# Gated-linear-attention heads in pairs and differential-attention maps in turns: matmuls that alternate between rows of the TensorE array

## The reference

```python
p = jax.nn.softmax(jnp.where(allowed, s, MASK_VALUE), axis=-1)
w = p[:, :, 0] - lam * p[:, :, 1]
return jnp.einsum('bhqk,bkhe->bqhe', w, v)
```

```python
decay = jnp.exp(jnp.where(causal[:, :, None], cum[:, :, :, None, :] - cum[:, :, None, :, :], NEG))
attn = jnp.einsum('bhik,bhjk,bhijk->bhij', qc, kc, decay)
o_intra = jnp.einsum('bhij,bhjv->bhiv', attn, vc)
...
merged = gates[:, :, 0, :] * (branches[0] @ w_branch[l, 0])
for n in range(1, N_BRANCH_2):
    merged = merged + gates[:, :, n, :] * (branches[n] @ w_branch[l, n])
```

## Time and profile before

| | |
|---|---|
| median of 3 runs | 2612.03 us (2608.58 to 2612.68) |
| the profiled execution | 2606.96 us, of which the span is 2605.2 us |
| PE matmul | 2459.5 us busy, 94% of the span, 18862 instructions |
| PE weight load | 2339.8 us, 90% |
| DVE | 1817.3 us, 70% |
| ACT | 1333.6 us, 51% |
| POOL | 419.9 us, 16% |
| mean granted TensorE clock | 0.972 |
| HBM read | 362.60 MB, 140 GB/s over the span |

### The profile page before, as it was taken

The page is one execution under the profiler, slowest core; times in us unless marked ns, Lnnn a source line. Parts: engine busy times, 40 slices in busy tenths (PEclk is TensorE's granted clock), DMA queues, the critical chain, the costliest instruction groups (busy, mean ns, idle before and its releaser), DMA issues.

```text
span 2605.2 us, 50262 instructions
## 1 busy us (share of the span) xinstructions
PE 2459.5 (94%) x18862; PEld 2339.8 (90%) x18862; DVE 1817.3 (70%) x3451; ACT 1333.6 (51%) x2218; POOL 419.9 (16%) x548
## 2 busy tenths in 40 slices
PE   7999998999999999998999998999999988999998
PEld 6998997888999998997888998888999988889998
DVE  5698855666875689856676774876766558667664
ACT  5644455755544644455755545544444454344443
POOL 0000003617930000003526940000000000000000
PEclk9999998999999999999999998988999999899999
DMA  5432342344554433342334554432545543334553
GB/s 208 161 107 100 112 147 88 114 138 146 170 171 156 167 113 109 106 146 98 114 133 151 171 178 138 146 114 90 170 158 182 186 140 128 101 118 146 195 186 130
DMA packets 100432, 366.76 MB, mean 141 GB/s; under 512 B 11632, under 2 KB 12144, under 8 KB 99824
## 3 DMA queue, kind: packets, MB, share of 16 engines
q1 hardware_dynamic: 100208, 363.69, 41.8%
HBM read 362.60 MB, written 1.05 MB: 140 GB/s over the span
## 4 chain that ended last, share of the span: by engine, by line
PE 58%; DVE 18%; POOL 9%; DVEq 5%; ACT 4%; issue 3%; ACTq 1%; DMA 1%; SPq 0%; POOLq 0%
PE psum L450 58%; POOL ring_lo L1963 9%; DVE ring_lo L1282 4%; ACT arena L852 2%; ACT ring_hi L865 1%; DVE arena L1316 1%; DVE arena L1324 1%; DMA ring<-w 1%; DVEq L1757 1%; DVE arena_r L1270 1%; DVEq L1262 1%; DVE arena_r L1268 1%; PE psum L527 1%; DVE arena L1414 1%; DVEq L1439 1%
## 5 line engine op out<-in xcount | busy, mean ns | idle before, releaser
L450 PE MATMUL psum<-hn_hi,ring_hi 128*128 128x272 f32 (+2 forms) x3936 | 1169.4, 298 | 46.6 <-ACT hn_hi L852 20.4
L450 PE MATMUL psum<-hn_hi,ring_lo 128*128 128x272 f32 (+2 forms) x3936 | 1138.3, 290 | 0.0
L450 PE MATMUL psum<-hn_lo,ring_hi 128*128 128x272 f32 (+2 forms) x3936 | 1103.4, 288 | 0.0
L450 PEld LDWEIGHTS psum<-hn_hi,ring_hi 128*128 128x128 f32 x3936 | 767.5, 195 | 79.8 <-issue 54.6
L865 ACT ACTIVATE ring_hi<-ring 128x1024 fp32r<-128x1024 f32 x684 | 715.0, 1055 | 231.0 <-DMA ring<-w 200.5
L1282 DVE TENSOR_TENSOR ring_lo<-ring,ring_hi 128x1024 fp32r<-128x1024 f32 x548 | 668.3, 1228 | 225.5 <-ACT ring_hi L865 187.0
L450 PEld LDWEIGHTS psum<-hn_hi,ring_lo 128*128 128x128 f32 x3936 | 767.3, 195 | 0.0
L450 PEld LDWEIGHTS psum<-hn_lo,ring_hi 128*128 128x128 f32 x3936 | 746.8, 193 | 1.7
L852 ACT ACTIVATE arena<-psum 128x272 f32<-128x272 f32 (+10 forms) x722 | 251.5, 366 | 707.9 <-PE psum L450 598.9
L1963 POOL TENSOR_TENSOR ring_lo<-ring,ring_hi 128x256 fp32r<-128x256 f32 x544 | 419.7, 808 | 1104.7 <-ACT ring_hi L865 1104.7
L450 PE MATMUL psum<-arena_r,ring_hi 128*128 128x256 f32 (+2 forms) x2996 | 555.2, 286 | 20.5 <-DVEq L1262 10.1
(11 more groups left out here) (154 smaller groups left out, 1463.7 us busy)
## 6 DMA issues: line engine op xcount, KB each, us to landing
ring<-w SPq DMA_DIRECT2D x684, 512.0 KB, 3.3
cst<-consts SPq DMA_DIRECT2D x1, 2120.0 KB, 14.6
x_sb<-x_meta SPq DMA_DIRECT2D x1, 1088.0 KB, 4.9
out<-x_sb SPq DMA_DIRECT2D x1, 1024.0 KB, 4.8
arena<-lam SPq DMA_DIRECT2D x1, 256.0 KB, 4.0
par_sb<-par SPq DMA_DIRECT2D x1, 193.0 KB, 4.8
pos_sb<-positions SPq DMA_DIRECT2D x1, 128.0 KB, 6.4
cst<-consts SPq DMA_DIRECT2D x1, 65.5 KB, 5.0
```

Source lines behind the costliest of these rows:

```text
L450: i = nc.tensor.matmul(out_, lhsT=lhsT, rhs=rhs, start=first, stop=last)
```

## The change

GLA's heads go in pairs. A new helper `side_by_side` takes the banks of both members first and then issues their matmuls in turns, part by part, so that neighbouring matmuls lie on different partitions. The merges move between the chunks: merge 4p after chunk 0 of both heads, merge 4p+1 after chunk 1 and the two cross products, merges 4p+2 and 4p+3 ahead of the two heads' values. ACT and DVE follow the same order; DVE calls `low` for merge 4p ahead of the first masked sum of a pair, and sums both heads' chunk 0, merges, then both heads' chunk 1. The scores of the first DSA head go ahead of merge 6 instead of merge 7. In the differential attention the two maps of a head take turns in the same way, the 16-row matmuls of both last. No matmul is added or left out. `level_parts` is `level_products` without the issuing.

```diff
+            def side_by_side(b, banks):
+                ps = [b.take(pe, key) for key, _ in banks]
+                for i in range(max(len(parts) for _, parts in banks)):
+                    for (key, parts), p in zip(banks, ps):
+                        if i < len(parts):
+                            rows, cols, lhsT, rhs = parts[i]
+                            mm(p[rows, cols], lhsT, rhs, True, True, b.filled(key) if i == len(parts) - 1 else None)
...
             def da_scores(h):
-                for m in range(2):
-                    q, k = DQ[64 * m:64 * m + 64, h, :], DK[64 * m:64 * m + 64, h, :]
-                    scores(b1, ("ds", h, m), [(slice(0, P), slice(0, P), q[:, 0:P], k[:, 0:P]),
-                                              (slice(0, P), slice(P, 3 * P), q[:, P:2 * P], k[:, 0:2 * P])])
-                    scores(b1, ("ds", h, 2 + m), [(slice(0, N_META), slice(0, T1), q[:, 2 * P:T1], k)])
+                maps = [(DQ[64 * m:64 * m + 64, h, :], DK[64 * m:64 * m + 64, h, :]) for m in range(2)]
+                side_by_side(b1, [(("ds", h, m), [(slice(0, P), slice(0, P), q[:, 0:P], k[:, 0:P]),
+                                                  (slice(0, P), slice(P, 3 * P), q[:, P:2 * P], k[:, 0:2 * P])])
+                                  for m, (q, k) in enumerate(maps)])
+                side_by_side(b1, [(("ds", h, 2 + m), [(slice(0, N_META), slice(0, T1), q[:, 2 * P:T1], k)])
+                                  for m, (q, k) in enumerate(maps)])
...
-                for g in range(GLA_HEADS):
-                    r = slice(32 * g, 32 * g + 32)
+                for p in range(GLA_HEADS // 2):
+                    pair = [(g, slice(32 * g, 32 * g + 32)) for g in (2 * p, 2 * p + 1)]
                     for t in range(2):
-                        level_products(b2, g, Z2[r, :, :], t, GQ[r, :], GK[r, :])
-                    scores(b2, ("cross", g), [(slice(0, P), slice(0, P), Z2[r, 3, 0:P], Z2[r, 3, P:T2])])
-                    merge2(0, 2 * g)
-                    if g == GLA_HEADS - 1:
+                        for n in range(2):
+                            side_by_side(b2, [level_parts(g, Z2[r, :, :], t, GQ[r, :], GK[r, :])[n] for g, r in pair])
+                        if t == 1:
+                            side_by_side(b2, [(("cross", g), [(slice(0, P), slice(0, P), Z2[r, 3, 0:P], Z2[r, 3, P:T2])]) for g, r in pair])
+                        merge2(0, 4 * p + t)
+                    if p == 1:
                         attention_scores("s", 0)
-                    merge2(0, 2 * g + 1)
-                    pe.wait_ge(*s2["att"].upto(g))
-                    values2("g", g, GV)
...
+                    for g, r in pair:
+                        merge2(0, 4 * p + 2 + g % 2)
+                        pe.wait_ge(*s2["att"].upto(g))
+                        values2("g", g, GV)
+                    sum_squares(b2, ("ssg", p), [SQ2[:, p, :]], T2, [s2["sqo"].upto(p)], ones64)
...
+                for p in range(GLA_HEADS // 2):
+                    pair = (2 * p, 2 * p + 1)
+                    low(b2, ("mB", 0, 4 * p), 2)
                     for t, cols in ((0, slice(0, P)), (1, slice(T2, T2 + P))):
...
+                        for g in pair:
...
+                            masked_sum(b2, ("lv", g, t), LT2, SS[:, g % 2, cols])
...
+                        merge_two(0, 4 * p + t)
+                    if p == 1:
                         attention_masked("s", 0)
...
+                    merge_two(0, 4 * p + 2)
+                    merge_two(0, 4 * p + 3)
```

More of the change, by code:

```diff
@@ L529, in transposes, with level_parts @@
                         t.then_inc(*b.filled(key))
-            def level_products(b, h, Zv, t, q, k):
+            def level_parts(h, Zv, t, q, k):
                 n = P if t < 2 else N_META
@@ L546, in level_products @@
                 if t < 2:
[L547 to L550, removed]
+                    return [(("lv", h, t, 0), parts[:1] + [part(0, 0, 64), part(1, 0, 32), part(1, 64, 32)] + parts[1:4]),
+                            (("lv", h, t, 1), parts[4:])]
+                return [(("lv", h, t, 0), parts)]
+            def level_products(b, h, Zv, t, q, k):
+                for key, parts in level_parts(h, Zv, t, q, k):
+                    scores(b, key, parts)
             def values_times_weights(b, key, V, base, cols, rows=slice(0, P), more=True):
@@ L1222, in _ @@
                 for g in range(GLA_HEADS):
[L1223 to L1224 removed]
+                    if g % 2 == 0:
+                        merge_sigmoid2(0, 2 * g)
+                        merge_sigmoid2(0, 2 * g + 1)
+                    merge_sigmoid2(0, 4 * (g // 2) + 2 + g % 2)
                     r = slice(64 * (g % 2), 64 * (g % 2) + 64)
@@ L1900, in _ @@
                         fence(s2["z"].done())
-                for g in range(GLA_HEADS):
-                    dve.wait_ge(*b2.full(("m", "o", 1) if g < 2 else ("g", "o", g - 2)))
+                for p in range(GLA_HEADS // 2):
+                    pair = (2 * p, 2 * p + 1)
+                    low(b2, ("mB", 0, 4 * p), 2)
                     for t, cols in ((0, slice(0, P)), (1, slice(T2, T2 + P))):
[L1905 to L1909, removed]
-                        attention_masked("s", 0)
[L1911 to L1921, removed]
@@ new lines, in _ @@
+                        for g in pair:
+                            if t == 0:
+                                dve.wait_ge(*b2.full(("m", "o", 1) if p == 0 else ("g", "o", g - 2)))
+                            masked_sum(b2, ("lv", g, t), LT2, SS[:, g % 2, cols])
+                            if t == 1:
+                                dve.wait_ge(*b2.full(("cross", g)))
+                                V.tensor_copy(SS[:, g % 2, P:T2], b2.of(("cross", g))[:, 0:P]).then_inc(*b2.free(("cross", g)))
+                                fence(s2["att"].done(g))
@@ new lines, in _ @@
+                        merge_two(0, 4 * p + t)
+                    if p == 1:
+                        attention_masked("s", 0)
+                    merge_two(0, 4 * p + 2)
+                    merge_two(0, 4 * p + 3)
+                    dve.wait_ge(*s2["rs"].upto(("ssg", p)))
+                    V.scalar_tensor_tensor(TP2[:, 1, 0:T2], GO[:, p, :], parb("ggla"), RS[:, 0:T2], ALU.mult, ALU.mult)
+                    V.drain()
+                    V.scalar_tensor_tensor(GG[:, p, :], GG[:, p, :], 0.5, TP2[:, 1, 0:T2], ALU.mult, ALU.mult)
@@ L1922, in _ @@
+                    V.drain()
+                    split(GG[:, p, :], GGS[0][:, p, :], GGS[1][:, p, :])
+                    fence(s2["normed"].done(p))
                 attention_combined("s", 0)
```

3 lines of the change are left out of this document (removed).

## The result

Before the change the runs timed beside it had a median of 2611.03 us (2608.58 to 2612.68, 4 runs), after it 2574.13 us (2570.13 to 2576.26, 4 runs). The ratio is 0.9859, with a 95% interval of 0.9844 to 0.9874: 36.9 us less. The prediction had 2573.5 us for the median and 2568.4 us for the profiled execution, which took 2575.9 us.

The account below looks back on a forecast made before the run. PE bounds the kernel with 58% of the chain of waits, DVE taking over in GLA once PE shortens. 2606.96 - 27.6 (GLA) - 11.0 (differential attention) = 2568.4 us profiled, plus 5.1 gives 2573.5 us median; range 2551 to 2590.

Parts of the forecast that it names:

- The pair at the time of one: GLA on PE: two heads in turns take one head's time, 4.34 us instead of 8.68, saving 8.7 us a layer.
- DVE becomes the bound in GLA: GLA stage: DVE's work and its root wait make 46.7 us against PE's 44.4, so DVE sets the end.
- the walk: GLA timeline from a pair's first product: normalising ends at 25.8 us, pair 1's masks start at 28.2, merge 6 at 37.9.
- Three terms of 48.8 us: GLA stage time: PE's 44.4 us, 3.05 us of holes and 1.3 us charged for half clock.
- The floor of PE: GLA: PE's own work at full clock, 53.1 us less 8.7 us for the pairs, is 44.4 us.
- The holes: GLA pair 1: PE waits for DVE to free banks, 1.85 us in chunk 0 and 1.2 us at merge 6.
- the total of 11.0 us: Differential attention: saving over both layers, 6.3 us in layer 0 and 4.7 in layer 1, limited by DVE's and ACT's round.
- the term of scores 2: Differential attention, third head: scores run at 1.2 GHz while DVE waits, so halving them saves 2.59 us a layer.
- A: Rival, chance 0.10: only PE counts in GLA and differential attention, saving 61.3 us, to 2550.8 us.
- B: Rival, chance 0.20: in GLA some eight PE waits each bring back a half-clock stretch, 1.7 us each; 2587 us.
- C: Rival, chance 0.05: in GLA and differential attention each strip change costs 0.12 us over 248 turns, no overlap; about 2636 us.
- D: Rival, chance 0.05: turns overlap nothing in either stage, only halved width changes gain, some 2 us; 2610 us.

Follow-up runs that it names:

- e3_no_turns: Changed kernel with pairs and new order kept, but a GLA pair's matmuls issued bank by bank instead of in turns; 2585.74 us in one run.
- e4_low_later: Changed kernel without the two slabs DVE makes ahead of each GLA pair; they are made at the pair's first merge; 2574.91 us in one run.
- e5_pool: Changed kernel with the low parts of five of a GLA stage's ten slabs moved from DVE to POOL; 2570.07 us in one run.
- e6_root_first: Changed kernel with ACT's last exponential tile of the next differential-attention head moved behind the previous head's root; 2560.83 us in one run.
- e1_gla_only: Changed kernel with the differential attention's scores as before, so the GLA pairs alone; 2580.27 us median, ratio to before 0.9883.
- e8_after_again: The changed kernel itself, unaltered, measured once more on another set of runs; 2570.71 us, ratio to before 0.9861.
- e2_da_only: Kernel before with only the differential attention's maps in turns, GLA as before; 2598.98 us, ratio to before 0.9954.
- e7_both: Changed kernel with five GLA low parts on POOL and ACT's last exponential tile behind the root; 2553.86 us, ratio to before 0.9800.

## Why the prediction was right

**The pair at the time of one, and the half clock.** Both nearly as read. 8.68 us became 4.60 (predicted 4.34), and e3_no_turns shows at one and the same clock what the turns do (3.67 against 2.41 us). The three quarters of ideal that the Trainium skill has for four strips (TensorE: Matmul & The Clock Gate, Part 3) would have made 5.6 us here, as an estimate from that page; two strips of 32 rows show 4.60. The clock stayed at 1.00 behind the pairs' runs of pair 0 and fell again only where PE had waited, 0.94 us for ACT's squares (L1247) or 1.5 to 2 us for DVE. Why thin runs bring it down isn't settled: a pair's run in turns is shorter than a head's and has 64 rows at work for 32. In e3_no_turns the half clock came behind a run of 3.45 us in pair 0 and not behind the next of 3.67 us.

**DVE becomes the bound in GLA.** Right for pair 1, from the root to merge 6, and to half a microsecond: by the walk pair 1's masks begin at t = 28.2 and merge 6 at 37.9; they came at 28.6 and 38.4. e4_low_later moved the hole and not merge 6, e5_pool moved merge 6 by one slab. Up to the root at 24.3 us PE and ACT set the pace, as in the walk (23.9).

**Three terms of 48.8 us were off and cancelled.** That the stage came within 0.35 us of the forecast is luck in this part. The floor of PE was 44.4 us in the sum and is 46.4 in the trace: 49.15 less the holes (0.27 + 0.94) and less 1.5 us for the half clock. I had taken a stretch's time by its mean clock, as if a microsecond at half clock cost half a microsecond. It costs less: a merge with 3.4 us at half clock takes 4.44 us and without 2.97, so 1.47 and not 1.7, and over the five such places of layer 0 before the 17.1 us of half clock cost 7.5 us. That makes 1.15 of the 2.0 us; 0.5 is the pair's 4.60 for 4.34. The remaining 0.35 is that a merge directly behind another takes 3.59 us from its first matmul to the next work's and one behind anything else 3.77: three of the eight stood behind another before, one does now. The holes were 1.85 + 1.2 in the sum and 0.27 + 0.94 in the trace, and the half clock was charged on top of them with 1.3. In truth they share the same time: when the half clock comes behind PE's wait for ACT's squares, on pair 1's first run and merge, PE is later there and the first hole is filled with slow work; when it doesn't, as in e6_root_first and e1_gla_only, the hole of 1.74 us is there (predicted 1.85), and the half clock lies on the next merge. Either way merge 6 begins at 38.4 to 38.95 us. So the true sum is 46.4 + 2.7 us for DVE's path, and the charge for the half clock is nearly nothing where DVE is the bound.

**The differential attention.** The mechanism holds, but the total of 11.0 us (12.7 measured) hides two errors that partly cancel. As predicted, 1.39 us came from head 0 in both layers, nothing from the stretch with the long wait (within 0.05 us), and PE's new wait is 1.30 us against about 1. Too small was the term of scores 2: from the values of head 0 to scores 3 the time fell by 4.8 us in layer 0 and 4.3 in layer 1, where 2.59 was counted. In this stretch the half clock lasted 5.6 instead of 13.2 us, and 3.4 instead of 9.8; I had counted the scores' own time at half clock, not that the clock is up again sooner for what follows. Too large was what comes behind: from scores 3 to the values of head 6 0.65 us in layer 0, where 1.4 and 0.9 of slack were counted, and 0.27 in layer 1 for 0.7. The round didn't stay at 14.56 us but grew to 14.73, so the slack wasn't paid out in full. The row at 534.13 from which the prediction read the round is a low part and not masked scores; it stands where the next ones would, and regular rounds of before are as long (14.56 to 14.59 us). e8_after_again has much the same stages (-6.9 and -5.9).

**DSA.** The 1.5 us of its first head weren't foreseen: 3.4 us of half clock are gone there in the changed kernel, in e1_gla_only and in e8_after_again. With e2_da_only they stay (29.85), and so they do in e6_root_first and e7_both (29.90, 29.83), which have the same GLA; so the change doesn't always bring them.

**The median.** The sum was carried from the profiled execution to the median with +5.1 us. For the profiled execution itself it was 7.5 us too low: the stages and DSA gave 2.5 us more than predicted, the rest took 10.2 us more. That the median was met to 0.6 us owes something to luck. The profile of before was indeed a short one: the medians of its runs lay at 2608 to 2611 us in three sets. The stages of this execution differ by 39.6 us and the medians by 36.9 and 37.6; the ranges of single runs (4 to 7 us) are as wide as that gap.

**The rivals.** A, PE alone counts (2550.8): false in both places by the waits of PE above, but e6_root_first shows what stands behind it, 23.2 us in the differential attention of the 25.0 counted for A. B, some eight half-clock stretches come back: one a stage did, and it cost next to nothing in the end. C, a change of strips costs 0.12 us, and D, nothing overlaps: refuted by the 2.19 and 2.41 us for two heads.

## What to carry to other kernels

Products of few contraction rows that lie on different rows of the array should be issued in turns, part by part, and not operand by operand: two of 32 rows took 1.06 times the time of one here and two of 64 rows the time of one, and the half clock behind the thin runs mostly went with it. Before counting such a gain in full, lay out the other engines' rounds in the same stretch: here DVE held GLA 2.7 us above PE, and in the differential attention one ACT instruction ahead of a root that DVE waited for held back some 10 us of the gain. Where another engine sets the end, a half clock on PE ahead of the wait for it costs nothing, so don't add it to that engine's path; behind the last such wait it does cost (1.5 us in e4_low_later). And relieve the other engine in the stretch that it bounds: low parts taken off DVE ahead of the root brought nothing.

## What the runs showed of the hardware

- Half a microsecond is too much for a microsecond at half clock: 0.43 here (1.47 us for a stretch of 3.4).
- The clock can fall behind one and the same 0.94 us wait of PE in one execution and not in the next: e5_pool has it in layer 0 and not in layer 1, e8_after_again for 3.4 us in layer 0 and for 6.8 in layer 1, at otherwise equal work.
- One head after the other on different strips still overlaps a little: 3.67 us for 40 matmuls, against 4.34 for 38 on one strip.
- A DVE operation with both inputs in SBUF mostly takes about twice its time beside POOL's subtraction, and one with an input in PSUM doesn't: 0.29 to 0.66 and 0.43 to 0.91 us against an unchanged 0.42 in e5_pool. Over the whole trace of the changed kernel the subtraction at L1287 on 272 columns has a median of 0.82 us in the 20 places that lie beside POOL and 0.44 in the 33 that don't. An operation of another form is hit too: the tensor-scalar at L1501 on 256 columns, with one input in SBUF besides its scalars, takes 0.86 and 0.35 us. But not every row is hit: L1441 at 533.55 in the kernel before lies beside POOL and takes 0.46.
